# A mix stage's output: the last convolution k tile of four tiles taken together, memory rows behind two output units, values' high halves in front of splits

## The reference

```python
h = rmsnorm(x, g_mix[l])
z = h @ w_mix_in[l]
zb, zc, zv, zq, zk, zval, zf = jnp.split(z, SPLITS, axis=-1)
y_conv = zb * causal_depthwise_conv(zc * zv, w_conv[l])
...
y_att = forgetting_attention(q, k, v, log_f)
y = jnp.concatenate([rmsnorm(y_conv, g_conv_out[l]),
                     rmsnorm(y_att, g_att_out[l])], axis=-1)
x = x + y @ w_mix_out[l]
x = x + memory_cross_attention(rmsnorm(x, g_xattn[l]), rmsnorm(mem, g_mem[l]),
                               w_xq[l], w_xkv[l], w_xo[l])
```

## Time and profile before

| | |
|---|---|
| Three runs | 3024.14, 3027.35, 3033.77 us; median 3027.35 |
| Profiled execution | 3027.2 us, of which the span from first to last instruction is 3025.4 |
| TensorE | busy 2927.3 us (97%), weight loads 2441.1 (81%) |
| VectorE, ScalarE, GpSimd | 1499.7 (50%), 1069.9 (35%), 819.0 us (27%) |
| Chain that ended last | TensorE 90%, VectorE 4%, GpSimd 2%, ScalarE 2% |
| Mean granted clock of TensorE | 0.983 of full speed |
| DMA | 84 GB/s read over the span |

### The profile page before, as it was taken

How to read it: one execution, slowest core, us unless ns; L and a number is a source line. 1 busy time by engine, 2 the same in 40 slices (tenths; PEclk the granted TensorE clock), 3 DMA queues, 4 the chain that set the end, 5 groups by cost and what they waited for, 6 DMA issues and landing times.

```text
span 3025.4 us, 35873 instructions
## 1 busy us (share of the span) xinstructions
PE 2927.3 (97%) x14832; PEld 2441.1 (81%) x14832; DVE 1499.7 (50%) x2055; ACT 1069.9 (35%) x1664; POOL 819.0 (27%) x446
## 2 busy tenths in 40 slices
PE   7999999899999999999999899999999999989989
PEld 6888888789888888888888789888888787777777
DVE  5554345454455534554345454455533666557653
ACT  3322234344333322332234444333223344344332
POOL 2000145364300001000145464300004544355432
PEclk8999999999999999999999999999999999999999
DMA  4332232133233232332332133233232211122111
GB/s 128 98 98 91 91 92 63 49 112 112 84 98 98 88 104 94 100 96 93 101 86 63 56 112 112 84 106 97 88 99 79 63 57 59 54 71 63 56 56 49
DMA packets 301362, 257.21 MB, mean 85 GB/s; under 512 B 10871, under 2 KB 299536, under 8 KB 301200
## 3 DMA queue, kind: packets, MB, share of 16 engines
q1 hardware_dynamic: 300880, 254.90, 27.2%
q0 software_dynamic: 320, 0.03, 0.0%
HBM read 252.79 MB, written 2.10 MB: 84 GB/s over the span
## 4 chain that ended last, share of the span: by engine, by line
PE 90%; DVE 4%; POOL 2%; ACT 2%; issue 1%; DMA 1%; SPq 0%; ACTq 0%; POOLq 0%; DVEq 0%
PE PS L1417 28%; PE PS L1419 27%; PE PS L1418 27%; PE PS L1423 2%; PE PS L1659 2%; POOL WL L2628 1%; PE PS L1664 1%; DVE WL L2119 1%; DVE AF L2534 1%; ACT WH L1772 1%; POOL SC L2636 0%; PE PS L1615 0%; PE PS L1506 0%; DMA SC<-in_consts_dram 0%; PE PS L1609 0%
## 5 line engine op out<-in xcount | busy, mean ns | idle before, releaser
L1417 PE MATMUL PS<-XH,WL 128*128 128x512 f32 x2256 | 903.8, 401 | 16.0 <-issue 8.9
L1419 PE MATMUL PS<-XH,WH 128*128 128x512 f32 x2256 | 885.5, 393 | 0.0
L1418 PE MATMUL PS<-XL,WH 128*128 128x512 f32 x2256 | 884.6, 392 | 0.0
L1772 ACT ACTIVATE WH<-RAW 128x1024 fp32r<-128x1024 f32 x448 | 465.7, 1044 | 1032.6 <-PE PS L1419 1001.0
L2119 DVE TENSOR_TENSOR WL<-RAW,WH 128x1024 fp32r<-128x1024 f32 (+1 forms) x296 | 388.1, 1314 | 496.9 <-ACT WH L1772 495.7
L2628 POOL TENSOR_TENSOR WL<-RAW,WH 128x1024 fp32r<-128x1024 f32 x184 | 445.1, 2427 | 477.1 <-ACT WH L1772 446.1
L1417 PEld LDWEIGHTS PS<-XH,WL 128*128 128x128 f32 x2256 | 427.7, 190 | 98.6 <-issue 15.7
L1419 PEld LDWEIGHTS PS<-XH,WH 128*128 128x128 f32 x2256 | 426.9, 189 | 92.6
L1418 PEld LDWEIGHTS PS<-XL,WH 128*128 128x128 f32 x2256 | 427.8, 190 | 81.8 <-issue 0.5
L1417 PE MATMUL PS<-AR,WL 128*128 128x512 f32 (+1 forms) x1216 | 469.2, 386 | 24.7 <-DVE AR L2364 7.5
L2636 POOL TENSOR_TENSOR SC<-SC 128x512 f32<-128x512 f32 x70 | 114.5, 1636 | 1315.0 <-ACT SC L1796 1310.3
(11 more groups left out here) (245 smaller groups left out, 3265.7 us busy)
## 6 DMA issues: line engine op xcount, KB each, us to landing
RAW<-in_w_ffn_gu_dram SPq DMA_DIRECT2D x176, 512.0 KB, 3.5
RAW<-in_w_ffn_down_dram SPq DMA_DIRECT2D x80, 512.0 KB, 3.4
RAW<-in_w_mix_in_dram SPq DMA_DIRECT2D x48, 512.0 KB, 3.8
RAW<-in_w_xkv_dram SPq DMA_DIRECT2D x32, 512.0 KB, 3.3
RAW<-in_a_w_in_dram SPq DMA_DIRECT2D x32, 512.0 KB, 4.0
RAW<-in_w_mix_out_dram SPq DMA_DIRECT2D x16, 512.0 KB, 3.5
RAW<-in_w_xq_dram SPq DMA_DIRECT2D x16, 512.0 KB, 3.3
RAW<-in_w_xo_dram SPq DMA_DIRECT2D x16, 512.0 KB, 3.3
```

Of the source, the lines that this page charges most:

```text
L1417: pe.matmul(o, ll, rh, start=start, stop=False, skip_group_check=skip)
L1418: pe.matmul(o, lh, rl, start=False, stop=False, skip_group_check=skip)
L1419: return pe.matmul(o, lh, rh, start=False, stop=stop, skip_group_check=skip)
L1772: act.activation(h, src, ACT.Copy).then_inc(sg["wh"].up(n))
```

## The change

It has three parts. In the output's first half, the k tiles 0, 1 and 2 of the four tiles 0 to 3 are computed first, then `ny_a`, then k tile 3 of these four, then `ny_b` and the closing of all four; tiles 4 to 7 follow as before, each closed right behind, and the step `mem_a` moves from behind tile 3 to behind tile 4. The side stream's rate goes from 4.5/40 to 4.5/44. In the order of units the two memory rows move from behind the first half's four units to behind the first two units of the second half. And in `values` (the mix stages, the differential and the last stage) the step that writes the high half of the second pair of row tiles stands ahead of the retiring of the two weight units, and so ahead of the splits that this sets off; in `rows_tile` the retiring moves behind the last product's tick.

```diff
--- before.py
+++ after.py
@@ -214,8 +214,9 @@
                     for p in range(4):
                         src = wo[u * 512:u * 512 + 512, p * 256:p * 256 + 256].rearrange("(k p) c -> p k c", p=128)
                         self.unit(((s, f"o{p}"), u), src)
-                    for r in range(0 if u else 2):
-                        self.unit(("mem", s, r), a["mem"][0, r * 128:(r + 1) * 128, :].rearrange("p (k c) -> p k c", c=128), kind="mem")
+                        if (u, p) == (1, 1):
+                            for r in range(2):
+                                self.unit(("mem", s, r), a["mem"][0, r * 128:(r + 1) * 128, :].rearrange("p (k c) -> p k c", c=128), kind="mem")
                 continue
             elif nm == "x":
                 wq, wkv, wo = a["w_xq"][l], a["w_xkv"][l], a["w_xo"][l]
@@ -548,9 +549,9 @@
             self.add("ny_b", (s, i), "yt", "yr")
             self.give(self.bank_of[s, "ny", i])
 
-        def half(m, u):
-            b = self.take()
-            yield from self.tile(((s, f"o{m // 2}"), 4 * u), b, m % 2)
+        def half(m, u, ks=None):
+            ch = (s, f"o{m // 2}"), 4 * u
+            yield from self.tile(ch, self.chunks[ch].banks[m % 2] if ks == (3,) else self.take(), m % 2, ks)
 
         def close(m, u):
 
@@ -597,18 +598,20 @@
         self.weave(self.flow(self.chain(self.values(s, 1), conv("c", 3), conv("v", 3), conv("b", 3))), side)
         self.finish(side)
         self.own_banks(0, 1, 2, 3, 4, 5)
-        side = self.stream(att(16, 19), 4.5 / 40)
-        for m in range(8):
+        side = self.stream(att(16, 19), 4.5 / 44)
+        for m in range(4):
+            self.weave(self.flow(half(m, 0, (0, 1, 2))), side)
+        ny_a(0)
+        for m in range(4):
+            self.weave(self.flow(half(m, 0, (3,))), side)
+        ny_b(0)
+        for m in range(4):
+            close(m, 0)
+        for m in range(4, 8):
             self.weave(self.flow(half(m, 0)), side)
-            if m == 1:
-                ny_a(0)
-            elif m == 3:
-                ny_b(0)
-                for i in range(4):
-                    close(i, 0)
+            close(m, 0)
+            if m == 4:
                 self.add("mem_a", (s,), "msq", "mms", "mpw", "mrow")
-            elif m > 3:
-                close(m, 0)
         self.finish(side)
         self.tick(99)
         for k2 in range(4):
@@ -918,7 +921,7 @@
                 self.retire(C.kmap[i][0], (ch, c, i))
             yield C.n // 256
 
-    def rows_tile(self, ch, n, bank):
+    def rows_tile(self, ch, n, bank, then=lambda: None):
 
         C = self.chunks[ch]
         C.banks[n] = bank
@@ -927,9 +930,12 @@
                 self.ready(C.kmap[k][0])
                 self.add("vmm", (ch, i, k), "mm")
                 if n == len(C.banks) - 1 and i % 2 and k == KT - 1:
+                    yield 1
+                    then()
                     for u in (C.kmap[0][0], C.kmap[k][0]):
                         self.retire(u, (ch, i, k))
-                yield 1
+                else:
+                    yield 1
 
     def own_banks(self, *banks):
 
@@ -988,9 +994,10 @@
         ch = ((s, f"v{c}"), 0)
         for n in range(2):
             b = self.take()
-            yield from self.rows_tile(ch, n, b)
+            yield from self.rows_tile(ch, n, b, (lambda: self.add("evh", (ch, 1), "vh")) if n else lambda: None)
             self.give(b, "evl", (ch, n))
-            self.add("evh", (ch, n), "vh")
+            if n == 0:
+                self.add("evh", (ch, n), "vh")
             self.later(5, "evl", (ch, n), "vl")
 
     def stick(self, s):
```

## The result

The changed kernel takes 3008.81 us (median of four runs, 3007.49 to 3012.46); the kernel before, run on the same chip, 3030.56. The ratio is 0.9932 with a 95% interval of 0.9910 to 0.9954: by the ratio 20.6 us, or 0.68%, faster. I had forecast 5 us and called "within 0.3%" the likeliest. The profiled execution of the changed kernel took 3007.49 us (span 3005.7), that of before 3027.2 (span 3025.4), so the two traces can explain 19.7 us.

The account below looks back on a forecast made before the run. TensorE, busy 97%, bounds the kernel through idling and low clock. Per mix stage 64.2 us work + 9.2 waits + 3.6 clock = 77.0 against 81.4 and 77.3; less 0.8, plus 1.15 (last stage): 5.1 gained, 3022 us, range 3011 to 3032.

Parts of the forecast that it names:

- within 0.3%: Whole kernel: time between 3018.3 and 3036 us, about 9 us either way being no change; chance 0.61.
- New waits in the mix stages: Each mix stage: waits of 2.5 us for attention row 15, 3.3 ahead of the fifth tile, 2.9 for the memory rows.
- Second half and second normalizers: Mix stages: wait for the second half's second unit (2.11 and 0.86 us) gone; second normalizers' wait 0.2 us.
- Clock in the mix stages: Each mix stage: low clock behind the new waits costs 3.6 us, from a mean of 1.46 over six waits.
- The other values: Differential stage, rest of last stage, memory values: no TensorE wait for L2242, nothing gained; bound -2 to +2 us.
- the sum: Mix stages: 77.0 us against 81.4 and 77.3, gains 4.4 and 0.3, less 0.8; last stage 1.15; 5.1 in all.
- What comes back as clock: Last stage: wait for the values ends some 1.15 us earlier; no clock gain counted there.
- The base: Whole kernel: the sum starts from the profiled execution of 3027.2 us, with the median of the runs at 3027.35.
- Short waits: Rival, mix stages: VectorE gets in first at the memory rows and TensorE stays at 2.4 GHz; 3011 us; chance 0.30.
- The low clock behind every wait: Rival, mix stages: three waits per stage each cost 2.85 us of clock, 10 us more, 3032 us; chance 0.12.

Follow-up runs that it names:

- e2 to e4: Against the kernel before, in turn: the new order of tiles alone, 3027.27 us; the new order of units alone, 3025.20; both together, 3023.87.
- e7: The kernel before plus one ScalarE copy of 768 columns ahead of the splits in the last stage's values: 3024.51 us, ratio 0.9974.
- e8: The kernel before with gain multiplications put out six counts later in all stages, nothing else changed: 3020.17 us, ratio 0.9957.

## Why the prediction was right or wrong

**New waits in the mix stages: right, to 0.5 us each.** 2.43, 3.11 and 2.45 us against 2.5, 3.3 and 2.9, and in e2 to e4 each appeared with the part that I had tied it to. That VectorE waits for whole instructions of GpSimd shows in 3.54 us for the scaling: of its two instructions the first took 2.88 us and ended 0.55 behind GpSimd's subtraction, the second took 0.74. The Trainium skill, "SBUF — State Buffer", section "Who interferes with whom", has it that between GpSimd and a VectorE instruction in a two-port mode whoever issues first holds the shared pair for the whole instruction: by that rule, the trace agrees (GpSimd at 605.60, VectorE at 605.66).

**Second half and second normalizers: right.** No wait for a unit there; forecast 0.2, measured none.

**Clock in the mix stages: mis-sized.** 3.6 us per stage forecast, from a mean over six waits; 3.3 in the first stage and 1.4 in the second measured. Together 2.5 us less clock and waits 1.0 us shorter in each stage turn 3.9 into 8.4; 0.8 were lost again at the wait in the cross attention, 7.1 is measured, and 0.5 stays unassigned. The same wait of 2.43 us left 3.1 us of low clock in the first stage and none in the second; what decides between them stays open.

**The other values: this is the step that failed.** 12.6 of the 19.7 us came from the differential and the last stage, where the sum has 1.15. I wrote "The other values ... cause no TensorE wait for L2242; I take nothing" with a bound of 2 us either way for a shift of 0.8 us "where VectorE queues behind a GpSimd subtraction". The sentence asked only which wait the moved instruction releases. It left out the splits, which move too, 0.8 us later, and what they set off: subtraction, free raw buffer, load, gain multiplication on GpSimd. This last lay 0.46 us ahead of a scan for which TensorE waits, a shift of 0.8 turned the two round, and each of the two waits lost 2.0 and 2.2 us. My bound of 2 us was the size of one such wait, and there are two, each with clock behind it. I had not gone through the waits of the last stage: behind the kernel's first 26 us the four longest are 4.53, which I did show, 4.51, 4.44 (for L2628 at 2659.97, which the change leaves) and 4.34. e7 shows the mechanism without the edit, e8 from the other side. In the differential stage the cause is plainer: VectorE stood 1.93 us for the high half (L1878) ahead of the attention's small operations, and no longer does; TensorE's wait of 2.55 for L1998 is 0.96. This is a wait for ScalarE, not for L2242, so that my sentence was true and still missed it; by the distances between the timelines it and the clock behind it are the whole of the 3.2 us there.

**What comes back as clock: mis-sized for the same reason.** I counted the last stage's gain as 1.15 us of wait. The three waits are 5.6 us shorter, and the stretches of low clock behind them cost 4.3 less, together 9.9 beside the 9.4 of the timelines. Where a wait is shortened, the clock behind it belongs to the sum; I had done this in the mix stages and not there.

**The base.** The sum was made against an execution of 3027.2 us; the median of 51 is 3032.7 (3030.56 for the four beside the change). This doesn't touch the 19.7 us between the traces, but it set the forecast's time 3 to 5 us low, while the missing gain set it high.

**The rivals.** "Short waits" has the time nearest to the measured one, 3011 beside 3008.81, and that is luck: VectorE did not get in first at the memory rows, and the clock stayed high behind one wait in four of those at row 15 and the fifth tile, not behind all. The low clock behind every wait did not come either. None of them lay outside the mix stages, and that is why the range ended at 3011: all its width came from one place.

## What to carry to other kernels

A reordering moves two things: the step that comes earlier and all that comes later for it. Follow the later one through its chain of buffers to the next load and to the engine behind that load, in every stage in which the edited function runs, and look there for a wait of the bound engine with two engines on one port. Where they start within a microsecond of each other, the price has two values far apart (here 2.0 us a time: 1.3 on the pair of scans, which waits for one GpSimd instruction more or less, and 0.7 on the subtraction behind it), not a small shift. List the longest waits of the whole kernel, whatever releases them, before deciding which stages an edit can't touch. And count expectations from the median of several executions, not from the one that was profiled.

## What the runs showed of the hardware

- Two scans of 512 columns on VectorE took 2.33 us with GpSimd idle, 3.99 where they started 0.34 us ahead of two GpSimd multiplications, and 5.29 where they started 0.46 us behind. GpSimd paid 5.33 in the second case and 4.67 in the third: the order decides who pays, and it pays to let the engine win for which TensorE waits. The whole difference between 3.99 and 5.29 is in the first scan of the pair, 1.22 against 2.52; the second took 2.86 and 2.85.
- Adding a 0.83 us copy to ScalarE made the kernel 7.9 us faster (ratio 0.9963 to 0.9986). It turned round such an order at two waits and shortened them by 4.25 us together.
- Of the 19.7 us between the traces about half (9.7) is TensorE's busy time, that is clock, and half (10.0) its idle time. Two waits of 2.43 us ahead of the same transposes left 3.1 us of low clock in one mix stage and none in the other.
- Where VectorE was released by a GpSimd operation and GpSimd's next one was ready, GpSimd was ahead in five places of the two mix stages, by 0.06 or 0.07 us (586.78, 1743.14 and 1766.01 before; 605.60 and 1741.79 after).
- Executions of the same program differ by the granted clock: 0.981 goes with 3034 to 3038 us, 0.985 with 3027 to 3031. The execution that was profiled lay 5.5 us below the median, more than the change's forecast gain.
